# The down projection of a two-layer decoder step on one core: plain products replaced by seven block products over blocks of middle channels

## The reference

```python
def conv_ffn(h, buf, w_gate, w_up, conv_w, conv_b, w_down):
    u = h @ w_gate                                   # 1024 -> 2816
    upad = jnp.concatenate([buf.astype(u.dtype), u], axis=1)
    c = conv_b + sum(conv_w[j] * upad[:, j:j + T] for j in range(CONV_W))
    y = (jax.nn.gelu(c) * (h @ w_up)) @ w_down       # 2816 -> 1024
    return y, upad[:, -(CONV_W - 1):]
# in the trunk:  x = x + rmsnorm(f, p['norm_ffn_post'][l])
```

## Time and profile before

| | |
|---|---|
| three runs | 1462.59, 1462.74, 1464.82 us; median 1462.74 |
| span of the profiled execution | 1460.7 us, 2.0 below the median of the runs |
| TensorE busy | 1424.8 us, 98% |
| VectorE / ScalarE / GpSimd busy | 910.8 / 676.9 / 562.9 us |
| 18 pairs of the second layer | about 1130 to 1316 us of the span |
| down projection of the second layer | about 1316 to 1450 us |
| down projection of the first layer | about 533 to 667 us |

### The profile page before, as it was taken

One profiled execution on the slowest core, in us unless ns is written; L12 is line 12 of the kernel. 1 busy time (PEld: TensorE's weight loads), 2 busy tenths in 40 slices (PEclk: granted clock), 3 DMA queues, 4 the chain that ended last, 5 costly groups with the idle time before them and its releaser, 6 DMA issues.

```text
span 1460.7 us, 31008 instructions
## 1 busy us (share of the span) xinstructions
PE 1424.8 (98%) x11156; PEld 1300.5 (89%) x11156; DVE 910.8 (62%) x1506; ACT 676.9 (46%) x1281; POOL 562.9 (39%) x552
## 2 busy tenths in 40 slices
PE   7999999999999999999999999999999999999997
PEld 6999999999999999998986666766989999999997
DVE  5732437599999992226457643443579999995323
ACT  5333345366666672216313544543275666665111
POOL 2342111145555553431330044441325655553433
PEclk9999999999999999999999999999999999999998
DMA  4243322222222333222321099981313222222231
GB/s 167 74 144 99 119 73 102 92 87 88 95 106 89 112 109 100 79 94 83 113 73 33 15 285 289 282 262 40 116 34 116 88 95 106 89 95 99 80 102 64
DMA packets 56714, 160.19 MB, mean 110 GB/s; under 512 B 7633, under 2 KB 27602, under 8 KB 55330
## 3 DMA queue, kind: packets, MB, share of 16 engines
q1 hardware_dynamic: 50466, 137.82, 28.3%
q0 software_dynamic: 6144, 20.98, 4.7%
HBM read 150.72 MB, written 8.05 MB: 109 GB/s over the span
## 4 chain that ended last, share of the span: by engine, by line
PE 45%; DVE 5%; issue 2%; ACT 1%; POOL 0%; SPq 0%; DMA 0%; POOLq 0%; ACTq 0%; DVEq 0%
PE lin L2287 15%; PE lin L2641 12%; PE lin L2859 4%; PE px L2898 2%; PE px L2936 2%; PE lin L2357 1%; PE px L2903 1%; PE px L2867 1%; PE px L2847 1%; PE lin L2813 1%; PE lin L2793 1%; PE px L2414 1%; PE px L2922 0%; PE lin L2830 0%; PE lin L2829 0%
## 5 line engine op out<-in xcount | busy, mean ns | idle before, releaser
L717 POOL TENSOR_TENSOR w_l<-w_raw,w_h 128x1408 fp32r<-128x1408 f32 (+1 forms) x50 | 143.9, 2878 | 271.6 <-ACT w_h L838 150.1
L712 POOL TENSOR_TENSOR w_l<-w_raw,w_h 128x1024 fp32r<-128x1024 f32 (+2 forms) x42 | 108.2, 2575 | 276.7 <-ACT w_h L838 266.9
L2287 PE MATMUL lin<-xg_h,w_h 128*128 128x272 f32 x848 | 194.1, 301 | 13.2 <-DVE xg_l L1458 10.6
L2287 PE MATMUL lin<-xg_l,w_h 128*128 128x272 f32 x848 | 183.5, 288 | 0.0
L2287 PE MATMUL lin<-xg_h,w_l 128*128 128x272 f32 x848 | 183.4, 288 | 0.0
L2641 PE MATMUL lin<-xq_h,w_h 128*128 128x272 f32 x576 | 166.4, 289 | 3.8 <-DVE xq_l L1844 2.2
L2641 PE MATMUL lin<-xq_h,wq_r 128*128 128x272 f32 x864 | 169.3, 289 | 0.6 <-ACT part L1133 0.6
L2641 PE MATMUL lin<-xq_h,w_l 128*128 128x272 f32 x576 | 166.0, 288 | 0.0
L2641 PE MATMUL lin<-xq_l,w_h 128*128 128x272 f32 x576 | 165.4, 287 | 0.0
L2287 PEld LDWEIGHTS lin<-xg_h,w_h 128*128 128x128 f32 x848 | 136.9, 189 | 20.8 <-issue 13.8
L838 ACT ACTIVATE w_h<-w_raw 128x1024 fp32r<-128x1024 f32 (+2 forms) x71 | 77.3, 1089 | 167.1 <-PE lin L2287 140.0
(11 more groups left out here) (407 smaller groups left out, 3231.4 us busy)
## 6 DMA issues: line engine op xcount, KB each, us to landing
wq_raw<-w SPq DMA_DIRECT2D x38, 1024.0 KB, 4.9
w_raw<-w SPq DMA_DIRECT2D x61, 512.0 KB, 3.5
w_raw<-w SPq DMA_DIRECT2D x30, 704.0 KB, 4.1
pages<-cache SPq DMA_DIRECT2D x128, 160.0 KB, 3.8
pages<-cache POOLq DMA_DIRECT2D x128, 160.0 KB, 3.9
St<-state SPq DMA_DIRECT2D x4, 1024.0 KB, 5.6
gla_s<-St SPq DMA_DIRECT2D x4, 1024.0 KB, 3.9
w_raw<-w SPq DMA_DIRECT2D x4, 576.0 KB, 3.6
```

The costliest lines, as they stand in the source:

```text
L712: g.tensor_tensor(w_l[:, p % 2, 0:n], raw_panel(p)[:, 0:n], w_h[:, p % 2, 0:n].bitcast(F32), ALU.subtract).then_inc(w_lo, 1)
L717: g.tensor_tensor(w_l[:, p % 2, 0:n], w_raw[:, p % 2, 0:n], w_h[:, p % 2, 0:n].bitcast(F32), ALU.subtract).then_inc(w_lo, 1)
L2287: last = mm(lin[:, 2 * out_set + half, 0:HALF], w[:, slot, (w0 + k) * P:(w0 + k + 1) * P], (v[ch] if isinstance(v, list) else v[:, ch, :]) ...
```

## The change

The down projection is cut along the middle channels into three blocks of 8, 6 and 8 chunks (`BLOCKS`: first chunk and half size: 0 and 4, 8 and 3, 14 and 4). For each block the output tiles are taken two at a time with the two halves of the tokens as a 2 x 2 block product in seven products, each of 4 x 3 matmuls (3 x 3 in the middle block). These are 11 more pairs behind the 18 (`d` = 0 to 10, `DOWN` = 11): four for block 0, four for block 1 and three for block 2. The last two output tiles of block 2 are done plainly (`last_down_tiles`). What the blocks give is summed in SBUF (`y_ffn`), by VectorE straight from PSUM (`down_a`, `down_b`, `down_c`) and by GpSimd from the parts that ScalarE copied out (`add_part`); the plain pair takes over the sum so far with one float32 product by the identity per tile and half (`so_far`).

A block needs seven operands of its own made from the middle activations: four sums (`mid_sum`, VectorE), seven rounded copies (`mid_hi`, ScalarE), remainders 1 to 4 (`mid_lo`, VectorE) and 0, 5, 6 (`mid_lo`, GpSimd). They go where the operands in use lie, so that operand n can be written only when product n of the last pair before the block is done. The operands of block 0 are written during the last gate and up pair (j = 17) and d = 0, those of block 1 during d = 3 and 4, those of block 2 during d = 7 and 8.

The core of the diff:

```diff
+BLOCKS = ((0, 4), (8, 3), (14, 4))
+DOWN = len(BLOCKS) * DC // 2 - 1
+ALL_PAIRS = PAIRS + DOWN
...
 # ScalarE
+                def mid_hi(b, n):
+                    low, high = mids(b)
+                    t1, t2, t3, t0 = mid_sums(b)
+                    q = BLOCKS[b][1]
+                    src = (low[:, :, first], t1, t2, t3, t0, high[:, :, first], high[:, :, second])[n]
+                    act.wait_ge(evac, ts_ + min(BLOCKS[b][0] + 2 * q - PLAIN, PAIRS))
+                    if 0 < n < 5:
+                        act.wait_ge(xt_done, SUMS * layer + 4 + 4 * b + n)
+                    act.wait_ge(w_used, used(pb + 4 * b - 1) + n + 1)
+                    fn(xq_h[n][:, 0:q], src, ACT.Copy, scale=-1.0 if n == 2 else 1.0).then_inc(op_h, 1)
...
+                for d in range(DOWN):
+                    j, (b, m) = PAIRS + d, block_of(d)
+                    last, turn = d == DOWN - 1, m == 3
+                    down_part(d, 0)
+                    quarter_hi(None, j, 6)
...
 # VectorE
+                    if turn:
+                        mid_lo(b + 1, 2)
+                    down_c(d)
+                    if turn:
+                        mid_sum(b + 1, 3)
+                    if not last:
+                        last_sum(None, j + 1)
+                        sum_lo(None, j + 1, 4)
+                    if turn:
+                        mid_sum(b + 1, 4)
+                        mid_lo(b + 1, 3)
...
 # TensorE, product n of a pair
-                    for k in range(4):
+                    q = 4
+                    if i is None and j >= PAIRS:
+                        b, m = block_of(j - PAIRS)
+                        q = BLOCKS[b][1]
+                    for k in range(q):
...
+                def so_far(m, half):
+                    mm(out(m, half), ident[:], y_ffn[:, DC - 2 + m, tok[half]], start=True, stop=False)
```

More of the change, by code:

```diff
@@ L749, in ffn, with pair @@
                 quarter_lo(None, 0, 3, A22, 4)
-                def pair(i, j, last=False):
+                def pair(i, j):
                     us1 = us0 + 3 * PLAIN
@@ L2023, in ffn @@
-                tile(None, 0)
-                with dve.Fori(0, DC // 2 - 1) as i:
-                    for m in (1, 2):
-                        tile(i, m)
-                if layer == 0:
-                    half_input(3, y_ffn, ("ffn_post", 0), range(0, AHEAD[3], 2))
-                    dve.wait_ge(sq_done, i0 + DC)
-                    tile(None, DC - 1, squares=False)
+                mid_sum(0, 3)
+                mid_lo(0, 2)
+                last_sum(None, j + 1)
+                sum_lo(None, j + 1, 4)
@@ L2345, in last_down_tile @@
                 pe.wait_ge(stat_ln, n)
                 ones_matmuls(flat(ssq[:]), True, False).then_inc(stat_ps, 1)
-                part(p + 1, high[-1:], len(high) - 1, 0, False, True).then_inc(h_tile, 1)
-                part(p, low[EARLY:EARLY + 2], EARLY, 1, False, False)
+                part(1, 0, 4, 6)
+                if both:
+                    pe.wait_ge(h_sq, first_halves(n) + 1)
+                    mm(px[:, 0, 0:HALF], ones[:], sq[:, (i - 1) % 2, first], start=False, stop=False)
@@ new lines, in last_down_tiles @@
+                part(1, 0, 6, DC).then_inc(h_tile, 1)
+                if both:
+                    part(0, 1, 2, 5)
+                    pe.wait_ge(h_sq, first_halves(n) + 2)
+                    mm(px[:, 0, 0:HALF], ones[:], sq[:, i % 2, first], start=False, stop=True).then_inc(h_sum, 1)
+                    part(0, 1, 5, DC).then_inc(w_used, 1)
+                    so_far(1, 1)
+                    part(1, 1, 0, 4)
+                    pe.wait_ge(sq_done, i)
+                    mm(px[:, 1, 0:HALF], ones[:], sq[:, (i - 1) % 2, second], start=False, stop=False).then_inc(sq_used, 1)
+                    part(1, 1, 4, DC).then_inc(w_used, 1)
+                    return
@@ L2706, in ffn @@
-                with pe.Fori(0, 2) as i:
-                    for m in (2, 3):
-                        whole_tile(i, m)
-                whole_tile(None, 6)
-                m = DC - 1
-                take_panel(pb + 2 * m)
-                free_set(tb_ + m)
-                last_down_tile(pb + 2 * m, tb_ + m, n_stat + 1, down(0), down(1))
+                for j in range(PAIRS - 1, ALL_PAIRS):
+                    pair(None, j)
+                pe.wait_ge(yp_done, adds_before(layer, 8))
+                pe.wait_ge(ya_done, 8 * (layer + 1))
```

628 lines of the change are left out of this document (414 added, 214 removed).

## The result

| | before | after |
|---|---|---|
| median of four runs, us | 1462.83 (1462.59 to 1464.82) | 1520.23 (1519.71 to 1521.29) |
| span of the profiled execution, us | 1460.7 | 1519.6 |
| TensorE's mean granted clock | 0.997 | 0.979 |

The changed kernel is slower: ratio 1.0392, 95% interval 1.0377 to 1.0406, some 57 us. The forecast was 1513, with a range of 1466 to 1535.

What follows compares the result with a forecast made beforehand. TensorE alone, busy 98%, was taken to set the time while others keep up. Span 1460.7 - 30.2 + 4.0 + 2.4 + 73.8 (waits) = 1510.7, in runs 1513 us; own range 1495 to 1530, with the weaker rival 1466 to 1535.

Steps and rivals of the forecast that it cites:

- TensorE's list shorter by 23.8 us: Whole kernel: 30.2 us of matmuls removed, less 4.0 for identity products and 2.4 at the end.
- The end, +2.4: Kernel end: fewer matmuls follow the first half's sum, and VectorE's normalisation delays the last products, adding 2.4 us.
- The turns: Where a block's operands are made: TensorE waits for the other engines, 16.3, 6.2 and 12.4 us per layer.
- The entrance: j = 17 and d = 0, making block 0's operands: TensorE waits 16.3 us per layer.
- the turn to block 1: d = 3 and 4, making block 1's operands: TensorE waits 6.2 us per layer.
- the turn to block 2: d = 7 and 8, making block 2's operands: TensorE waits 12.4 us per layer.
- The walk through the three lists: Down projection: VectorE, ScalarE and GpSimd operations timed one by one, VectorE and GpSimd taking turns; waits of 36.9 us per layer.
- my walk without the exclusion: The three turns if VectorE and GpSimd do not exclude each other: waits of 19.2 us per layer.
- Other, 2.0 per layer: Other down-projection waits: 1 us for the pairs with q = 3, 1 us for d = 9, 10 and last weights.
- 0.1257 us a matmul in between: Sign expected in the profile after: between TensorE's waits, matmuls keep stepping at 0.1257 us.
- the weaker form: Rival, chance 0.25: VectorE and GpSimd do not exclude each other, only VectorE–ScalarE hand-overs cost; 1477 us in runs (1466 to 1495).
- the gain arrives: Rival, chance 0.15 wholly or in part: the other engines keep up, TensorE never waits; 1439 us, faster.

Runs made afterwards that it cites:

- x_none: Changed kernel with most of the block sums, remainders, rounded copies and GpSimd's down-projection work cut to a few columns, TensorE's list kept: 1444.77 us.
- x_nopool: Changed kernel with only GpSimd's remainders and additions in the down projection cut to a few columns: 1490.35 us.
- x_fill: Changed kernel plus 196 matmuls per layer into unused accumulator columns, in front of the five long waits: 1518.11 us.
- x_nosum: Changed kernel with VectorE's block sums and remainders cut to 32 of 272 columns, ScalarE copying a middle activation in place of the sum: 1496.16 us.
- x_noturn: Changed kernel with the making of all blocks' operands cut to 32 of 272 columns (16 on GpSimd), the pairs' other work whole: 1462.36 us.

## Why the prediction was right, step by step

- **TensorE's list shorter by 23.8 us.** Nearly: `x_none` is 17.9 us under the span before. The 5.9 between are in part the short waits that are left in it (2.8 us for parts, of which 0.6 stand in the kernel before too, and 0.5 for `y_ffn`), and in the first layer four more records of squares' sums ahead of the end (ten instead of six, 0.25 each); the rest I did not take apart.
- **The end, +2.4.** The last sum of squares begins at 1506.91, and the end is 12.7 behind it; before it began at 1450.54 (the same time as the copy in the earlier trace rows), 10.2 ahead of the end. 2.5 measured.
- **The turns.** The entrance costs 15.5 us per layer by the table (15.59 less the 0.13 it had at j = 16) for 16.3; the turn to block 1 22.46 - 15.59 = 6.9 for 6.2; the turn to block 2 34.33 - 23.19 = 11.1 for 12.4. Where I took the first wait for 6.2 us before product 6 of j = 17 and the second for 5.5 before product 2 of d = 0, 6.0 and 4.4 stand in the profile. The walk through the three lists with the lock of VectorE and GpSimd in it was right in mechanism and place, and in its sum. That the sum came so near was partly luck. In `x_nopool`, where GpSimd's share is cut, the three turns still cost 10.1, 6.3 and 7.6 us per layer by the same measure, 24.0 in all, where my walk without the exclusion gave 19.2. The hand-overs between VectorE and ScalarE cost more than I took, and GpSimd's share less: 9.5 us of the three turns in place of 15.7. The two errors offset each other.
- **Other, 2.0 per layer.** The step that failed: 5.1 by the table, 0.7 at d = 7, 3.5 at d = 10 and 0.8 at the plain pair. I had counted VectorE's time in the steady pairs and not GpSimd's chain of two remainders, the extra operand's first, in front of an addition that ScalarE waits for.
- **No term for the clock.** By luck of the method it needed none. The walk fixed the times at which the others release TensorE, and these hold whatever TensorE's speed between them (`x_fill`); the waits in the profile (28.9 + 28.4 = 57.3) are shorter than the lateness of 76.8, of which the slower steps at 1.2 GHz take 18.2; the rest, some 4 us after the short waits of `x_none` are taken off, are the first matmuls behind a wait and small gaps. What I had named as a sign, 0.1257 us a matmul in between, did not hold behind the long waits: 0.226.

The sum: 38.55 per layer for 36.9 is +3.3 in two layers, the list is +5.9 longer: 9.2 against the 8.9 by which the span of 1519.6 exceeds my 1510.7. Of the rivals, the weaker form is refuted by `x_nopool`'s durations, "the gain arrives" by the changed kernel itself. My later idea that VectorE's sums were the cause fell with `x_nosum`, and that the clock cost 20 us of time fell with `x_fill`, though the slow steps do add up to 18. What `x_noturn` adds, and what I had not seen: even without the turns this order of the lists had no gain to give.

## What to carry to other kernels

Before work is taken off an engine that is busy all the time, walk through the lists of the others in the new stage, operation by operation, with their waits for one another and the VectorE and GpSimd operations that exclude each other one after the other; that gave three turns within 2 us each, partly by errors that offset each other, where busy shares over the whole span said nothing. When several lists are full at once, the releaser that the profile names is only the last in a queue of equals: the two new orders tried here moved the waits, and less work on any one of the three engines shortened them. A low clock behind a wait need not be a loss: here the next product would only have waited again.

## What the runs showed of the hardware

- A matmul at the lower of the two clock levels steps in 0.226 us where it steps in 0.1257 at the higher, and keeping TensorE multiplying through the waits kept the granted clock at 1.00 (mean 0.996 in `x_fill`, 0.979 in the changed kernel).
- The price of the exclusion is not a share but a queue: the same VectorE sum takes 0.69 us alone, 1.54 beside the rest of a GpSimd remainder of 512 elements, and 3.04 beside one of 1088 (2.99); both times it ends 0.56 us behind GpSimd's. Operations of 128x512 with an operand in PSUM never took more than 0.70 (L2012 and L2027), beside GpSimd's or not.
- Starting products in columns 272 to 511 of a PSUM bank while a sum in columns 0 to 271 was open changed what the kernel gives (`x_fill`). The Trainium skill, PSUM — Partial Sum Buffer, "The four PSUM rules", says that the first matmul of a group clears the written-marks of the whole 2 KiB bank, whichever columns it writes; the run agrees, but none tells the start from the mere writing.
